# The low part of a weight piece on GpSimd: four instructions of a quarter of the columns in place of one

## The chip, the cores and the metric

The kernel runs on one core of one Trainium2 chip. The metric is the device time of one execution in microseconds (us), as the median of several runs. Engine names follow the profile: PE is TensorE's matmul, PEld its weight load, DVE is VectorE, ACT is ScalarE, POOL is GpSimd, SP is SyncE.

## The reference

256 tokens of width 1024 pass through one hybrid block (gated linear attention beside sliding-window attention, then a SwiGLU layer) and two more layers (latent attention beside an HGRN2 scan, then a dense SwiGLU in the first and a top-2-of-8 mixture of experts in the second). Cut to what matters here, the work is a chain of products with large weights, all in float32:

```
proj = h @ w_in[l]                      # 1024 x 6688, later 1024 x 2752 in each of two layers
y    = o_gla @ w_o_gla, o_swa @ w_o_swa, merged @ w_out
x    = x + (silu(h2 @ w_gate) * (h2 @ w_up)) @ w_down
...
f = lb + (1.0 - lb) * jax.nn.sigmoid(z)
log_f = jnp.log(jnp.maximum(f, F_FLOOR))
```

## The kernel before, in words

**Three passes for a float32 product.** A weight w is split into a high part, w rounded to the fp32r type, and a low part, w minus the high part. The left side is split in the same way, and PE adds up three products (L726 high by high, L727 high by low weight, L728 low by high weight). One *piece* is 128 partitions by 1024 words, as a rule two blocks of 512 columns; PE multiplies it in 12 matmuls.

**Who does what for a piece.** SP loads a weight block of 2048 words into one of four slots of the tile `arena`. ACT copies a piece to `w_hi_sb` (function `split_to`, L1519), after PE has counted up `w_used` for the piece four places before, since `w_hi_sb` and `w_lo_sb` have four buffers. Then the low part is made: on DVE for the first pieces and for nearly all of the two SwiGLU stages (L1983) and the experts (L1971), and on POOL (L655) for the 134 pieces of the mixers and of the joins between stages. PE waits for the counter of the piece (`lo_count`) before its first matmul. So a piece of the mixers goes SP, ACT, POOL, PE, and POOL may be at most three pieces ahead of the one that PE works on.

**What else the engines do there.** DVE and ACT run the elementwise work of the mixers in an order written out by hand. ACT's copies stand in that order too: behind an activation that waits for DVE, the next piece's high part waits as well. The steps which the prediction names are, in the first block, L2050 and L2069 to L2072 (rotation and norms of the attention's heads; ACT's L1573 waits for L2050), and in the two later layers the forget gate: L1938, L2356 and L2357 in the first of them, L1938, L2361, L1926, L2364, L2365, L2366, L2368 and L2370 in the second. There PE's L1137 (the running sum of the log gates) waits for L2368, PE's L860 (the turned keys) for L2370, and ACT's L1714 for L2365, with four copies of weight pieces behind it.

**The loop on POOL.** After its small loads POOL goes through the pieces with one wait and one instruction each:

```
w = raw(j)
k, n = w.shape[1:]
pool.wait_ge(sem("w_hi_ready"), hi_count[j])
pool.tensor_tensor(buffer(w_lo_sb, j, k, n), w, buffer(w_hi_sb, j, k, n).bitcast(F32),
                   ALU.subtract).then_inc(sem("w_lo_by_gpsimd"), 1)
```

Of the kernel before, what the change touches and what calls it, by code (L numbers as in the profile page):

```python
# [28 lines left out]
ALU = mybir.AluOpType  # L29
ACT = mybir.ActivationFunctionType  # L30
F32 = mybir.dt.float32
# [36 lines left out]
MOE_SUBS = 2 * MOE_LOADS  # L68
FF_UNIT = 256
FFN_UNITS = D_FF // FF_UNIT  # L70
SCRATCH = 4 * SLOT
WORK = 13952

# [113 lines left out]
def build(nc, A, out):  # L187
    gemm_at, jobs = {}, 0
    for name, _, _, width, _ in gemm_plan():
        if name in ("FFN", "lr"):  # L190
            continue
        halves = [name.replace("wo", f"wo{i}") for i in range(2)] if width == D else [name]
        for part in halves:
            gemm_at[part], jobs = jobs, jobs + T
    pair_at, pair_end, n = {}, {}, 0
# [16 lines left out]
    for name, weight, start, width, k in gemm_plan():  # L212
        if name != "FFN":
# [15 lines left out]
            else:  # L229
                n = KD if KD * width <= SUB else KD // 2  # L230
# [3 lines left out]
        down = A[f"{weight}_down"].rearrange("(k p) n -> p k n", p=P)  # L234
        for u in range(FFN_UNITS + 1):
            if u < FFN_UNITS:
                for kind in ("gate", "up"):
# [16 lines left out]
    for j, (_, _, piece) in enumerate(subs):  # L254
        by_vector = j < FIRST_SUBS or any(lo + BUFFERS <= j < hi + AFTER_FFN for lo, hi in ffn_range.values())
        maker = "w_lo_by_vector" if by_vector else "w_lo_by_gpsimd"
        if piece is not None:
            made["w_hi_ready"] += 1
            made[maker] += 1
        hi_count.append(made["w_hi_ready"])  # L260
        lo_count.append((maker, made[maker]))
# [3 lines left out]
    for j, (i, _, piece) in enumerate(subs):  # L265
        load_freed[i] = lo_count[j] if piece is not None else ("w_used", j + 1)

    with ExitStack() as ctx:
        sems = {}

        def sem(name):
            if name not in sems:
                sems[name] = ctx.enter_context(nc.semaphore(name))
            return sems[name]

        def sb(name, words, dtype=F32):
            return ctx.enter_context(nc.sbuf_tensor(name, [P, words], dtype))


        arena = sb("arena", DENSE_SLOTS * SLOT + SCRATCH + WORK)  # L280
        x_sb = sb("x_sb", T * D)
        h_sb = sb("h_sb", T * D)
        left_sb = sb("left_sb", 2 * KD * TOKENS, F32R)
        w_hi_sb, w_lo_sb = (sb(f"w_{n}_sb", BUFFERS * SUB, F32R) for n in ("hi", "lo"))
# [8 lines left out]
        def room(at, words):  # L293
            assert at + words <= SCRATCH + WORK
            at += DENSE_SLOTS * SLOT
            return arena[:, at:at + words]

        def work(at, words):
            assert at + words <= WORK
            at += DENSE_SLOTS * SLOT + SCRATCH  # L300
            return arena[:, at:at + words]

        def scratch(at, words):
            assert at + words <= SCRATCH
            return arena[:, DENSE_SLOTS * SLOT + at:DENSE_SLOTS * SLOT + at + words]
# [13 lines left out]
        def raw(j):  # L319

            i, _, piece = subs[j]
            return piece_of(slot(slot_of[i], *loads[i][1:]), piece)

        def buffer(store, j, k, n):

            at = (j % BUFFERS) * SUB
            return store[:, at:at + k * n].rearrange("p (k n) -> p k n", k=k)
# [120 lines left out]
        def wide(u):  # L448
            return 2 <= u < FFN_UNITS - 1

        def added_ahead(tag):
            return (FFN_UNITS - 3) * (tag == "f2")

# [166 lines left out]
        def _(pool):  # L620
# [29 lines left out]
            for j, (_, _, piece) in enumerate(subs):  # L650
                if piece is not None and lo_count[j][0] == "w_lo_by_gpsimd":
                    w = raw(j)
                    k, n = w.shape[1:]
                    pool.wait_ge(sem("w_hi_ready"), hi_count[j])
                    pool.tensor_tensor(buffer(w_lo_sb, j, k, n), w, buffer(w_hi_sb, j, k, n).bitcast(F32),  # L655
                                       ALU.subtract).then_inc(sem("w_lo_by_gpsimd"), 1)

            pool.wait_ge(sem("expert_gain_landed"), 16)
            for half in range(2):
# [63 lines left out]
        def _(pe):  # L723
# [308 lines left out]
            def ffn(tag, norm, turn_next):  # L1032
# [54 lines left out]
                def banks_free(u, kind):  # L1087
# [3 lines left out]
                    elif wide(u):  # L1091
                        pe.wait_ge(sem(("gate_added", "up_added")[kind]), added_ahead(tag) + u - 2)
                    elif u == FFN_UNITS - 1 and kind == 0:
                        pe.wait_ge(sem("gate_added"), added_ahead(tag) + u - 2)

                for u in range(FFN_UNITS):
                    if u == 0:
# [1619 lines left out]
```

## Time and profile before

| | |
|---|---|
| median of 3 runs | 1897.99 us (1897.94 to 1900.1) |
| the profiled execution's own time | 1899.83 us |
| span of its instructions | 1897.9 us |
| PE busy | 1875.3 us (99%) |
| DVE busy | 1523.3 us (80%) |
| ACT busy | 1240.1 us (65%) |
| POOL busy | 403.3 us (21%) |
| mean granted TensorE clock | 0.999 |

The span is from the first to the last instruction of the profiled execution. An engine's busy time counts an instruction from its start to its end, and what it spends waiting for access to memory inside the instruction counts as busy. Matmul ends are modelled, so that PE's small gaps tell more than its share. POOL works on weight pieces from 28.7 us to 278 us, from 460 to 606 us and from 787 to 922 us; in between and after that DVE makes the low parts.

### The profile page before, as it was taken

What the parts mean: (1) busy time and instruction counts of PE and PEld (TensorE: products, weight loads), DVE (VectorE), ACT (ScalarE), POOL (GpSimd) and SP (SyncE); (2) the same over time, 40 slices, a digit from 0 to 9 for tenths busy, and PEclk for the clock granted to TensorE, in tenths of its full rate; (3) what the DMA queues carried; (4) which work ended last, traced back from release to release, by engine and by line L of the source; (5) the groups of instructions that cost most, each with busy time, mean ns of one, the idle gap of its engine ahead of it and who ended that gap; (6) DMA issues with size and microseconds to landing.
All of it is one profiled execution on the core that took longest, in us unless ns stands there. A gap on an engine that the chain in (4) does not pass through costs nothing.

```text
span 1897.9 us, 26327 instructions
## 1 busy us (share of the span) xinstructions
PE 1875.3 (99%) x9450; PEld 1578.4 (83%) x9450; DVE 1523.3 (80%) x1649; ACT 1240.1 (65%) x1484; POOL 403.3 (21%) x206
## 2 busy tenths in 40 slices
PE   9999999999999999999999999999999999999997
PEld 6888888888898888878888888888888888888886
DVE  6745367777576887697699999999999999999997
ACT  6654444444644444464488888888888888888876
POOL 6856870001824000282450000000000000000000
PEclk9999999999999999999999999999999999999999
DMA  9534556665434676534599999999999999999994
GB/s 284 170 119 134 178 186 218 224 221 172 142 122 133 206 242 221 163 120 134 176 383 395 391 380 376 386 397 368 389 365 388 396 365 388 366 387 396 370 395 188
DMA packets 251397, 523.68 MB, mean 276 GB/s; under 512 B 9944, under 2 KB 58720, under 8 KB 251184
## 3 DMA queue, kind: packets, MB, share of 16 engines
q1 hardware_dynamic: 243408, 504.00, 74.2%
q10 hardware_dynamic: 5680, 11.61, 1.7%
q0 software_dynamic: 2224, 6.95, 1.1%
q8 instruction: 52, 0.85, 0.2%
q14 instruction: 33, 0.27, 0.0%
HBM read 507.19 MB, written 15.34 MB: 275 GB/s over the span
## 4 chain that ended last, share of the span: by engine, by line
PE 93%; DVE 3%; POOL 1%; ACT 1%; issue 1%; DMA 0%; SPq 0%; DVEq 0%; ACTq 0%
PE bank L726 25%; PE bank L728 24%; PE bank L727 24%; PE bank L1081 6%; PE bank L1084 3%; PE bank L1160 2%; POOL w_lo_sb L655 1%; PE bank L849 1%; PE bank L1345 1%; PE bank L822 1%; PE bank L828 1%; DMA arena<-in_w_in 0%; PE bank L990 0%; PE bank L967 0%; DVE arena L2050 0%
## 5 line engine op out<-in xcount | busy, mean ns | idle before, releaser
L1971 DVE TENSOR_TENSOR w_lo_sb<-arena,w_hi_sb 128x1024 fp32r<-128x1024 f32 x672 | 807.8, 1223 | 73.8 <-ACT w_hi_sb L1499 43.6
L1499 ACT ACTIVATE w_hi_sb<-arena 128x1024 fp32r<-128x1024 f32 x672 | 711.2, 1062 | 168.7 <-PE bank L728 168.0
L726 PE MATMUL bank<-w_hi_sb,left_sb 128*128 128x512 f32 (+1 forms) x1400 | 553.4, 395 | 2.8 <-POOL w_lo_sb L655 2.8
L728 PE MATMUL bank<-w_hi_sb,left_sb 128*128 128x512 f32 (+1 forms) x1400 | 542.3, 387 | 0.0
L727 PE MATMUL bank<-w_lo_sb,left_sb 128*128 128x512 f32 (+1 forms) x1400 | 541.5, 387 | 0.0
L1519 ACT ACTIVATE w_hi_sb<-arena 128x1024 fp32r<-128x1024 f32 (+1 forms) x269 | 278.2, 1052 | 299.8 <-PE bank L728 220.8
L655 POOL TENSOR_TENSOR w_lo_sb<-arena,w_hi_sb 128x1024 fp32r<-128x1024 f32 (+1 forms) x134 | 341.6, 2569 | 552.0 <-ACT w_hi_sb L1519 551.2
L726 PEld LDWEIGHTS bank<-w_hi_sb,left_sb 128*128 128x128 f32 x1400 | 263.1, 188 | 61.1 <-POOL w_lo_sb L655 7.6
L728 PEld LDWEIGHTS bank<-w_hi_sb,left_sb 128*128 128x128 f32 x1400 | 262.9, 188 | 54.9
L727 PEld LDWEIGHTS bank<-w_lo_sb,left_sb 128*128 128x128 f32 x1400 | 263.4, 188 | 50.9 <-issue 0.7
L726 PE MATMUL bank<-w_hi_sb,hid_hi_sb 128*128 128x512 f32 x656 | 257.3, 392 | 0.1
L727 PE MATMUL bank<-w_lo_sb,hid_hi_sb 128*128 128x512 f32 x656 | 255.6, 390 | 0.0
L728 PE MATMUL bank<-w_hi_sb,hid_lo_sb 128*128 128x512 f32 x656 | 255.5, 389 | 0.0
L1983 DVE TENSOR_TENSOR w_lo_sb<-arena,w_hi_sb 128x1024 fp32r<-128x1024 f32 x135 | 160.4, 1217 | 77.8 <-ACT w_hi_sb L1519 76.7
L710 POOL DMA_INDIRECT h_sb<-returned,arena x2 | 2.7, 1356 | 819.7 <-DMA returned<-arena 819.4
L728 PEld LDWEIGHTS bank<-w_hi_sb,hid_lo_sb 128*128 128x128 f32 x656 | 123.1, 188 | 25.9
L726 PEld LDWEIGHTS bank<-w_hi_sb,hid_hi_sb 128*128 128x128 f32 x656 | 123.3, 188 | 24.9 <-DVE w_lo_sb L1971 0.5
L727 PEld LDWEIGHTS bank<-w_lo_sb,hid_hi_sb 128*128 128x128 f32 x656 | 123.3, 188 | 24.2
L1081 PE MATMUL bank<-left_sb,w_hi_sb 128*128 128x512 f32 x512 | 127.8, 391 | 0.0
L1081 PEld LDWEIGHTS bank<-left_sb,w_hi_sb 128*128 128x128 f32 x512 | 93.1, 189 | 17.3
L1926 DVE TENSOR_TENSOR arena<-arena 128x512 f32<-128x512 f32 (+3 forms) x85 | 80.6, 948 | 27.0 <-ACT arena L1530 20.9
L1084 PEld LDWEIGHTS bank<-left_sb,w_lo_sb 128*128 128x128 f32 x512 | 69.8, 190 | 6.4 <-DVE w_lo_sb L1983 1.4
(356 smaller groups left out, 1687.5 us busy)
## 6 DMA issues: line engine op xcount, KB each, us to landing
arena<-in_moe_w_gate SPq DMA_DIRECT2D x112, 1024.0 KB, 7.9
arena<-in_moe_w_up SPq DMA_DIRECT2D x112, 1024.0 KB, 8.0
arena<-in_moe_w_down SPq DMA_DIRECT2D x112, 1024.0 KB, 7.7
arena<-in_w_in SPq DMA_DIRECT2D x45, 1024.0 KB, 5.1
arena<-in_w_ffn_in SPq DMA_DIRECT2D x22, 1024.0 KB, 5.1
arena<-in_w_out SPq DMA_DIRECT2D x12, 1024.0 KB, 5.1
arena<-in_w_ffn_out SPq DMA_DIRECT2D x11, 1024.0 KB, 4.8
arena<-in_dense_w_gate SPq DMA_DIRECT2D x11, 1024.0 KB, 5.4
```

The source lines that it names most:

```text
L655: pool.tensor_tensor(buffer(w_lo_sb, j, k, n), w, buffer(w_hi_sb, j, k, n).bitcast(F32), ALU.subtract).then_inc(sem("w_lo_by_gpsimd"), 1)
L726: pe.matmul(out, still[0], moving[0], start=start, stop=False)
L727: pe.matmul(out, still[0], moving[1], start=False, stop=False)
L728: return pe.matmul(out, still[1], moving[0], start=False, stop=stop)
L1081: pe.matmul(sums, w_hi[:, k, :], left_both[:, :, k, :], start=(k == 0), stop=False)
L1084: mm = pe.matmul(sums[:, 0, :], w_lo[:, k, :], left_hi[:, k, :], start=False, stop=(k == KD - 1))
L1160: mm = pe.matmul(b[:, i * P:(i + 1) * P], key[:, at:at + P], query[:, at:at + P], start=True, stop=True)
L1499: act.activation(expert_buffer(w_hi_sb, j), expert_piece(j % MOE_SUBS), ACT.Copy) \
L1519: act.activation(buffer(w_hi_sb, j, *w.shape[1:]), w, ACT.Copy).then_inc(sem("w_hi_ready"), 1)
L1926: dve.tensor_tensor(dst, one, two, ALU.mult).then_inc(sem(name), 1)
L1971: dve.tensor_tensor(expert_buffer(w_lo_sb, j), expert_piece(j % MOE_SUBS), expert_buffer(w_hi_sb, j).bitcast(F32), ALU.subtract) \
L1983: dve.tensor_tensor(buffer(w_lo_sb, j, *w.shape[1:]), w, buffer(w_hi_sb, j, *w.shape[1:]).bitcast(F32), ALU.subtract) \
```

## The change

`LO_CUTS = 4` is new. In POOL's loop the last dimension of a piece, n, is cut into four steps, and each step gets a subtraction of its own on the same slices of `w_lo_sb`, `arena` and `w_hi_sb`. The wait stands before the first of the four, and the counter `w_lo_by_gpsimd` goes up with the last. Nothing else changes.

```
+LO_CUTS = 4
...
                     pool.wait_ge(sem("w_hi_ready"), hi_count[j])
-                    pool.tensor_tensor(buffer(w_lo_sb, j, k, n), w, buffer(w_hi_sb, j, k, n).bitcast(F32),
-                                       ALU.subtract).then_inc(sem("w_lo_by_gpsimd"), 1)
+                    step = n // LO_CUTS
+                    for at in range(0, n, step):
+                        lo, whole, hi = (a[:, :, at:at + step] for a in (buffer(w_lo_sb, j, k, n), w, buffer(w_hi_sb, j, k, n)))
+                        ins = pool.tensor_tensor(lo, whole, hi.bitcast(F32), ALU.subtract)
+                    ins.then_inc(sem("w_lo_by_gpsimd"), 1)
```

POOL's program before, where its loads end and the pieces begin (a row is a line of the kernel, an operation, out<-in, the shape, and how many follow each other):

```order
L626 DMA level_masks<-in_level_masks 128x1024
L655 ISA
L655 TENSOR_TENSOR w_lo_sb<-arena,w_hi_sb 128x1024 x88
L655 TENSOR_TENSOR w_lo_sb<-arena,w_hi_sb 128x768 x2
L655 TENSOR_TENSOR w_lo_sb<-arena,w_hi_sb 128x1024 x30
```

The same place in the changed kernel, where the line is L659:

```order
L627 DMA level_masks<-in_level_masks 128x1024
L659 ISA
L659 TENSOR_TENSOR w_lo_sb<-arena,w_hi_sb 128x2x128 x280
L659 TENSOR_TENSOR w_lo_sb<-arena,w_hi_sb 128x8x32 x16
L659 TENSOR_TENSOR w_lo_sb<-arena,w_hi_sb 128x2x128 x56
L659 TENSOR_TENSOR w_lo_sb<-arena,w_hi_sb 128x4x48 x8
L659 TENSOR_TENSOR w_lo_sb<-arena,w_hi_sb 128x2x128 x48
```

Each piece has become four instructions, 134 pieces 536 of them, of two blocks of 128 columns as a rule; no other engine's instructions move.

## Rows read from the trace of the kernel before

**Rows 1.** The page: the span, busy times (share, count), POOL's and ACT's piece lines.

```profile
span 1897.9 us, 26327 instructions
...
PE 1875.3 (99%) x9450; PEld 1578.4 (83%) x9450; DVE 1523.3 (80%) x1649; ACT 1240.1 (65%) x1484; POOL 403.3 (21%) x206
...
L1519 ACT ACTIVATE w_hi_sb<-arena 128x1024 fp32r<-128x1024 f32 (+1 forms) x269 | 278.2, 1052 | 299.8 <-PE bank L728 220.8
L655 POOL TENSOR_TENSOR w_lo_sb<-arena,w_hi_sb 128x1024 fp32r<-128x1024 f32 (+1 forms) x134 | 341.6, 2569 | 552.0 <-ACT w_hi_sb L1519 551.2
```

**Rows 2.** Waits: who waited for whom, us in total, times, longest.

```profile
PEld bank L726 <- POOL w_lo_sb L655: 7.6, 11, 1.8
...
PE bank L726 <- POOL w_lo_sb L655: 2.8, 5, 1.4
```

**Rows 3.** Timeline of POOL (start, us, engine, line, [idle before]): long instructions, no DVE between.

```profile
28.69 9.44 POOL L655 TENSOR_TENSOR w_lo_sb<-arena,w_hi_sb 128x1024 fp32r<-128x1024 f32 x4
...
1887.14 2.52 POOL L718 TENSOR_TENSOR arena<-x_sb,arena 128x512 f32<-128x512 f32 x2 [86.67 <-DVE x_sb L2630]
```

**Rows 4.** Groups of lines: POOL's memset; timeline of POOL: an add of two columns.

```profile
L2695 POOL MEMSET const-float32-1.0<- 128x1 f32 x1 | 0.1, 98 | 0.0
...
944.02 0.20 POOL L680 TENSOR_TENSOR arena<-arena 128x2 f32<-128x2 f32 x1
```

**Rows 5.** Timeline of the second later layer's forget gate, 799 to 823 us.

```profile
799.73 14.77 POOL L655 TENSOR_TENSOR w_lo_sb<-arena,w_hi_sb 128x1024 fp32r<-128x1024 f32 x5
...
808.94 3.32 DVE L1926 TENSOR_TENSOR arena<-arena,const_sb 128x1024 f32<-128x1024 f32 x1
...
811.13 3.37 POOL L655 TENSOR_TENSOR w_lo_sb<-arena,w_hi_sb 128x1024 fp32r<-128x1024 f32 x1
...
812.30 3.29 DVE L2364 SCALAR_TENSOR_TENSOR arena<-arena,const_sb 128x1024 f32<-128x1024 f32 x1
...
814.56 0.50 PE L726 MATMUL bank<-w_hi_sb,left_sb 128*128 128x512 f32 x1 [0.32 <-POOL w_lo_sb L655]
...
818.05 1.23 DVE L2368 TENSOR_TENSOR arena<-arena 128x1024 f32<-128x1024 f32 x1
819.19 3.40 DVE L2370 TENSOR_TENSOR arena<-arena 128x1024 f32<-128x1024 f32 x1
...
819.33 2.05 PE L1137 MATMUL bank<-const_sb,arena 128*128 128x128 f32 x16 [1.73 <-DVE arena L2368]
822.64 0.33 PE L860 MATMUL bank<-const_sb,arena 128*128 128x128 f32 x1 [1.26 <-DVE arena L2370]
```

**Rows 6.** Timeline of the first later layer's forget gate, 470 to 489 us.

```profile
470.58 24.84 POOL L655 TENSOR_TENSOR w_lo_sb<-arena,w_hi_sb 128x1024 fp32r<-128x1024 f32 x9 [6.04 <-ACT w_hi_sb L1519]
...
473.70 0.50 PE L726 MATMUL bank<-w_hi_sb,left_sb 128*128 128x512 f32 x1 [0.39 <-POOL w_lo_sb L655]
...
485.03 3.37 POOL L655 TENSOR_TENSOR w_lo_sb<-arena,w_hi_sb 128x1024 fp32r<-128x1024 f32 x1
...
488.46 0.50 PE L726 MATMUL bank<-w_hi_sb,left_sb 128*128 128x512 f32 x1 [0.32 <-POOL w_lo_sb L655]
```

**Rows 7.** Timeline of the first block's start, 32 to 53 us.

```profile
32.18 6.51 DVE L2050 TENSOR_SCALAR arena<-arena 128x1024 f32<-128x1024 f32 x1
...
43.33 20.00 POOL L655 TENSOR_TENSOR w_lo_sb<-arena,w_hi_sb 128x1024 fp32r<-128x1024 f32 x7 [5.20 <-ACT w_hi_sb L1519]
...
45.95 0.50 PE L726 MATMUL bank<-w_hi_sb,left_sb 128*128 128x512 f32 x1 [1.42 <-POOL w_lo_sb L655]
...
52.10 0.50 PE L726 MATMUL bank<-w_hi_sb,left_sb 128*128 128x512 f32 x1 [0.31 <-POOL w_lo_sb L655]
```

**Rows 8.** Busy times in a stretch: us, PE, PEld, DVE, ACT, POOL (count), clock, DMA.

```profile
206.00:278.00 72.00, 72.00 (x355) 60.33 (x353) 33.69 (x33) 33.59 (x43) 63.20 (x25) 1.00 0.53 179
```

**Rows 9.** Chain of waits: one matmul of a piece, when nothing holds PE up.

```profile
580.14 0.23 PE bank L728
```

**Rows 10.** Timeline: a tiny POOL instruction beside low parts on DVE.

```profile
956.81 5.06 POOL L680 TENSOR_TENSOR arena<-arena 128x2 f32<-128x2 f32 x1
...
957.19 4.62 DVE L1971 TENSOR_TENSOR w_lo_sb<-arena,w_hi_sb 128x1024 fp32r<-128x1024 f32 x4
```

## The prediction, before the changed kernel had run

> **What bounds the kernel now.** I read the page first [rows 1]: PE is busy for 1875.3 of 1897.9 us, POOL for only 21%. So the time is PE's own work plus its gaps, and the change, which touches POOL alone, counts only where it opens or closes a gap in PE. The list of waits comes next [rows 2]: PE and its weight loads wait for POOL's low part L655 for 2.8 and 7.6 us, at some ten places, so POOL is late now and then. The mean of L655 is 2569 ns [rows 1], but a piece with no DVE work beside it takes less: four in a row take 9.44 us, 2.36 each [rows 3]. What lies between is the thing to see, and the timeline shows it. In the forget gate of the last layer a POOL piece takes 3.37 us and DVE's 1024-column instructions with two operands in SBUF take 3.29 to 3.40 us, where the same kind (L2368), met when POOL is idle, takes 1.23 [rows 5]. The sums fit taking turns: 3.29 is 1.2 of its own and 2.1 of waiting for the end of POOL's instruction; 3.37 is 2.36 and 1.0 of waiting for DVE's. So such instructions of DVE and POOL's shut each other out, whole instruction by whole instruction. The last thing to see is where PE starts a piece the moment POOL ends it: at 45.95 and 52.10 us [rows 7], at 473.70 and 488.46 us, where the piece that began at 485.03 with 3.37 us ends at 488.40 [rows 6], and at 814.56 us, where the row 799.73 + 14.77 ends at 814.50 [rows 5]. There anything added to POOL is added to PE.
>
> **Price of the four instructions.** Two L718 of 512 columns take 2.52 us, 1.26 each, against 2.36 for 1024 [rows 3]: 1.10 us for 512 columns is 2.15 ns a column, which leaves 0.16 us for the instruction itself. A quarter then takes 256 x 2.15 ns + 0.16 = 0.71 us, and a piece 2.84: **0.48 us more**. The bounds: from the memset of one column, 0.10 us, three more give +0.30; from the add of two columns, 0.20 us, +0.60 [rows 4]. Below that lies nothing added, if quarters without a wait between them run into each other; no row excludes it. I take 0.48, since L718 is the nearest in kind and size. As for the page: the Trainium skill (GPSIMD Engine Reference, Elementwise — side-by-side cycle accounting) gives 4497 ns for 2048 columns. With the 2.36 us of this trace that would be 2.09 ns a column and an estimated 0.22 us an instruction, so +0.67 us a piece and an estimated 3.4 us more over the 18 or so late pieces below than by my price.
>
> **Where it is hidden.** 134 pieces x 0.48 = 64 us more of POOL, nearly all beside other work. PE needs 12 x 0.23 = 2.7 us a piece [rows 9]. POOL may be three pieces ahead: after PE frees a buffer, ACT takes 1.05 us [rows 1] and POOL 2.4, and PE gets there three pieces later, 8.2 us, so the lead is 4.7 us. The tightest long stretch is 206 to 278 us with POOL busy for 63.2 of 72 us in 25 pieces [rows 8]. 25 x 0.48 = 12 makes that 75.2, 3.2 us too many, inside the lead: nothing. At +0.60 it is 78.2, and 1.5 us would show. If that cover is gone, every further 0.1 us per piece costs 2.5 us here.
>
> **Place A, first block.** POOL's four first pieces end at 38.13 (28.69 + 9.44), and DVE's L2050, which wanted in at 32.18, ends at 38.69 [rows 3, 7]; ACT behind it and then the piece that POOL begins at 43.33 wait on that. If L2050 stays out until POOL is through again, all of this comes 4 x 0.48 = 1.9 us later, and the three pieces until PE's start at 52.10 add 1.4: +3.3. If it gets in between quarters, POOL is no longer idle from 38 to 43 us, but has seven pieces in a row, 7 x 2.84 = 19.9 from 28.69, and the turns of L2050, L2069 to L2072 of both halves inside them (1.0 each for 1024 columns, about 0.5 for 512 and for L2050, some 6.5 in all by then): 55.1 instead of 52.05, +3.0. Both come to about **+3**.
>
> **Place B, first later layer.** Six pieces between POOL's start at 470.58 and 488.41, each of them awaited by PE or nearly so [rows 6]. DVE's turns there stay the same in number, so 6 x 0.48 = **+2.9**.
>
> **Place C, second later layer.** Six pieces end at 814.50, the five of the row and one directly before it, with three turns of DVE in them [rows 5]. Now L2364 and what is behind it (L2365, L2366, L2368, L2370) wait 0.7 us at most each instead of 2.1, so DVE runs its chain some 3 us sooner. But POOL then still has its pieces to do and gives a turn of 1.0 us to each: five turns that used to fall into POOL's pause fall into its work. The last of the six pieces ends 6 x 0.48 + 5 x 0.98 = 7.8 us later, at 822.3. PE takes 2.7 us for it and starts L1137 at 825.1 instead of 819.33; its own wait of 1.73 us for L2368 is gone, and so is that of 1.26 for L2370 before L860, which starts at about 827.0 instead of 822.64: **+4.4**. What is late next here is POOL, no longer DVE. ACT's copies behind L1714 come sooner, but POOL has no time for them.
>
> **Sum.** 3.0 + 2.9 + 4.4 = +10.3 us, after 922 us nothing. On the profiled execution's own 1899.83 that is 1910.1; that execution lies 1.8 above the median of the runs, so on the median's 1897.99 it is **1908.3 us**. With +0.30 a piece the same working gives 2.1 + 1.8 + 3.3 = 7.2, with +0.60 it gives 4.2 + 3.6 + 5.1 + 1.5 = 14.4.
>
> **Rival 1: POOL does not let DVE in between quarters** that follow each other without a wait. For it: DVE does just this to POOL when its instructions overlap; an add of two columns stood for 5.06 us beside four of DVE's [rows 10]. Against it: POOL's pieces of before follow each other without a pause too, and DVE gets in between them [rows 5]. Then A costs 3.3 and B 2.9. At C four instructions of DVE on the chain wait 0.48 longer, and L860 comes 2.4 us later: +8.6, 1906.6 us.
>
> **Rival 2: the extra price is near nothing and only the turns move.** Then A and B cost under 1, and C 5 x 0.98 less the 3.0 us that PE stood for DVE: +1.9. In all about +2.5, 1900.5 us, no change that can be told. Against it stands L718.
>
> **Rival 3: faster, because DVE is freed.** The waits of 2.1 us in DVE's chain at C shrink to 0.7 and the one of 5.9 in L2050 at A goes. If POOL kept its pace, PE would lose its gaps of 1.73 and 1.26 at C and 1.42 and 0.31 at A: -4.7, 1893.3 us. It decides at C: the sixth piece must be done 2.7 us before 819.33, by 816.6, which leaves 2.1 us for six times the extra price and five turns. It speaks for it that ACT's copies wait on this chain too; against it that turns alone take 4.9. The Trainium skill has a rule for this (SBUF — State Buffer, Who interferes with whom): a DVE instruction with two SBUF inputs contends with a reading GpSimd instruction, and who holds the pair has it for its whole instruction. By that rule shorter instructions free DVE sooner, as here; the trace agrees on the whole instruction (3.29 us beside POOL, 1.23 without it).
>
> **Rival 4: a quarter costs more than 0.85 us**, so that a piece takes 3.4 and POOL cannot keep up from 206 to 278 us: A 6, B 6, C 8 and 25 x 1.0 + 63.2 - 72 - 4.7 = 12 there: +32 or less. Only strided quarters could do that; no row shows it.
>
> **Chances.** My sum, +5 to +15: 0.66. Rival 1: 0.12. Rival 2: 0.12. Rival 3: 0.06. Rival 4: 0.04. A measurement of this kernel can tell about 0.2%, 3.8 us, from no change. Slower by more than that: 0.66 + 0.12 + 0.03 of rival 4, less a little for a sum at its lower bound, 0.79. Within it: rival 2 and the rest, 0.15. Faster: 0.06. The range that holds it 8 times in 10 goes from rival 2's 1900.0 to 1915.0, a little above the upper bound of the price.
>
> **What would show it.** Right: 536 instructions of L659 with 0.7 us each where DVE is idle, start to start, 2.8 us a piece; waits of PE for POOL up from 10 to some 20 us; L2364 and L2370 at 1.3 to 1.9 us in place of 3.3; the waits of L1137 and L860 for DVE gone; PE's start after the sixth piece at C about 14 us behind its old place when A and B are counted (3 + 2.9 + 7.8). Wrong: PE waiting for POOL no longer than before, quarters start to start at 0.6 us, or DVE's instructions still at 3.3 us, which would be rival 1.

## The result, and the profile after

The changed kernel takes **1930.7 us**, the median of four runs (1927.1 to 1940.9), against 1898.0 for the kernel before (1897.9 to 1900.1): the ratio is 1.0177, with a 95% interval from 1.0162 to 1.0192. That is 32.7 us slower, where 10.3 were predicted; the time lies outside the range. The profiled execution is the fastest of the four, 1927.1 us. In what follows, line numbers from 655 on stand 4 higher in the changed kernel than in the kernel before (L655 is L659, L1926 is L1930), and 3 to 9 higher in the kernels of the experiments (L1926 is L1929 to L1935 there).

The page first, the lines that answer to [rows 1]:

```profile
span 1925.1 us, 26729 instructions
...
PE 1882.7 (98%) x9450; PEld 1582.9 (82%) x9450; DVE 1510.7 (78%) x1649; ACT 1241.0 (64%) x1484; POOL 467.6 (24%) x608
...
L730 PE MATMUL bank<-w_hi_sb,left_sb 128*128 128x512 f32 (+1 forms) x1400 | 555.4, 397 | 12.8 <-POOL w_lo_sb L659 12.7
...
L659 POOL TENSOR_TENSOR w_lo_sb<-arena,w_hi_sb 128x256 fp32r<-128x256 f32 (+1 forms) x536 | 406.0, 799 | 515.1 <-ACT w_hi_sb L1523 515.0
```

POOL's low parts grew from 341.6 to 406.0 us, by 64.4, where 64 was predicted. That the two agree so closely is partly luck: the price measured below, 0.42 us a piece, gives 56 for 134 pieces, and the other 8 were not traced. The span grew by 27.2, though, and PE is busy for 7.4 us longer with the same 9450 matmuls. The waits (who, for whom, us in total, times, longest) show a line that has no counterpart in [rows 2]:

```profile
PEld bank L730 <- POOL w_lo_sb L659: 20.6, 18, 3.1
...
PE bank L730 <- POOL w_lo_sb L659: 13.7, 12, 2.7
...
PE bank L730 <- DVE hid_lo_sb L1960: 7.7, 1, 7.7
```

The waits for POOL went from 10.4 to 34.3 us and not to 20, and there is one wait of 7.7 us for **DVE**, on which nothing in the prediction rests. Where it comes from is seen in the timelines of POOL and of DVE around it (start, us, engine, line, [idle before]):

```profile
209.77 31.25 POOL L659 TENSOR_TENSOR w_lo_sb<-arena,w_hi_sb 128x256 fp32r<-128x256 f32 x45
...
220.94 21.16 DVE L1930 TENSOR_TENSOR arena<-arena 128x1024 f32<-128x1024 f32 x1 [5.06 <-ACT arena L1534]
242.14 0.69 DVE L1959 CAST hid_hi_sb<-bank 128x512 fp32r<-128x512 f32 x1
242.86 0.69 DVE L1960 TENSOR_TENSOR hid_lo_sb<-bank,hid_hi_sb 128x512 fp32r<-128x512 f32 x1
...
245.04 1.22 DVE L1930 TENSOR_TENSOR arena<-arena 128x1024 f32<-128x1024 f32 x1
```

One DVE instruction that takes 1.22 us by itself stands for 21.16 us. The quarters of POOL follow each other without a pause, the 45 shown and 27 before them, until 241.02, and the instruction ends 1.1 us after that: it was passed over at 29 ends of a quarter, one after the other, and let in after the row's last. The same happened at 512 us to two instructions of L2399 (9.49 us instead of 1.29), and there PE waited for the DVE copy behind them:

```profile
512.15 9.49 DVE L2399 TENSOR_TENSOR arena<-arena 128x512 f32<-128x512 f32 x2
521.56 1.40 DVE L1926 COPY arena<-bank 128x512 f32<-128x512 f32 x2
523.00 1.29 DVE L2399 TENSOR_TENSOR arena<-arena 128x512 f32<-128x512 f32 x2
...
523.02 3.22 PE L1164 MATMUL bank<-arena 128*128 128x128 f32 x14 [3.48 <-DVE arena L1926]
```

The last piece is the clock. In the kernel before it is at 1.00 until 1890 us. In the changed kernel it is not (us, busy times of PE, PEld, DVE, ACT and POOL with counts; then the granted clock of TensorE, the DMA share, GB/s):

```profile
230.00:235.00 5.00, 5.00 (x24) 4.14 (x23) 5.00 (x1) 3.10 (x4) 5.00 (x8) 1.00 0.56 210
235.00:240.00 5.00, 1.02 (x5) 0.52 (x3) 5.00 (x1) 1.06 (x1) 5.00 (x8) 0.99 0.65 209
240.00:245.00 5.00, 1.30 (x3) 1.14 (x4) 4.86 (x5) 0.00 (x0) 1.02 (x2) 0.50 0.55 176
245.00:250.00 5.00, 5.00 (x20) 3.98 (x20) 1.23 (x2) 1.06 (x1) 0.67 (x1) 0.83 0.09 34
250.00:255.00 5.00, 5.00 (x24) 4.14 (x23) 1.96 (x2) 3.10 (x4) 5.00 (x7) 1.00 0.00 0
...
520.00:530.00 10.00, 6.98 (x32) 6.38 (x33) 8.04 (x11) 5.03 (x8) 3.23 (x5) 0.83 0.19 60
...
830.00:840.00 10.00, 5.23 (x15) 3.50 (x13) 9.27 (x6) 4.62 (x6) 10.00 (x7) 0.83 0.33 105
840.00:850.00 10.00, 10.00 (x49) 8.60 (x50) 1.38 (x2) 3.68 (x4) 10.00 (x15) 0.83 0.34 88
```

While PE stands still for 7.7 us, the granted clock falls to 0.50, the lower of its two levels (1.2 GHz). It is there by 240 us and stays until 3 us after PE's start at 243.70, and in these 3 us a matmul takes 0.43 us in the chain of waits instead of the 0.23 of [rows 9]:

```profile
245.32 0.43 PE bank L730
...
247.18 0.23 PE bank L732
```

Setting each matmul's start beside the same one's before gives the account of the 27.1 us by which PE ends later (rounded): place A 2.9; the stretch from 206 to 300 us 10.0 (a gap of 7.8, 1.5 of half clock, and 0.7 at its end); place B 2.6; L2399 and the half clock behind it 5.4; place C 5.5; after it 0.8. The three places of the prediction sum to 11.0.

Place C, to be set beside [rows 5]:

```profile
829.37 1.65 DVE L1930 TENSOR_TENSOR arena<-arena,const_sb 128x1024 f32<-128x1024 f32 x1
831.05 1.63 DVE L2368 SCALAR_TENSOR_TENSOR arena<-arena,const_sb 128x1024 f32<-128x1024 f32 x1
...
837.62 1.75 DVE L2374 TENSOR_TENSOR arena<-arena 128x1024 f32<-128x1024 f32 x1
...
833.32 0.50 PE L730 MATMUL bank<-w_hi_sb,left_sb 128*128 128x512 f32 x1 [2.69 <-POOL w_lo_sb L659]
840.00 0.50 PE L730 MATMUL bank<-w_hi_sb,left_sb 128*128 128x512 f32 x1 [2.08 <-POOL w_lo_sb L659]
847.16 1.95 PE L1141 MATMUL bank<-const_sb,arena 128*128 128x128 f32 x16
848.94 1.04 PE L864 MATMUL bank<-const_sb,arena 128*128 128x128 f32 x8
```

Here DVE does what was predicted (3.3 us shrank to 1.6 to 1.75), L1141 and L864 no longer wait for it, and PE waits for POOL instead.

### The profile page after: what moved, and what is told of

It reads as the page before. It is cut to its first block, busy times and chain, and to the rows that moved or that the text cites. A ratio compares the mean times of both kernels' runs of the same rounds, so it can differ in the third digit from the quotient of the medians.

```text
span 1925.1 us, 26729 instructions
## 1 busy us (share of the span) xinstructions
PE 1882.7 (98%) x9450; PEld 1582.9 (82%) x9450; DVE 1510.7 (78%) x1649; ACT 1241.0 (64%) x1484; POOL 467.6 (24%) x608
## 4 chain that ended last, share of the span: by engine, by line
PE 87%; POOL 6%; DVE 4%; ACT 1%; issue 1%; DMA 0%; SPq 0%; DVEq 0%; ACTq 0%; POOLq 0%
PE bank L730 23%; PE bank L732 23%; PE bank L731 23%; PE bank L1085 6%; POOL w_lo_sb L659 5%; PE bank L1088 3%; PE bank L1164 1%; DVE arena L1930 1%; PE bank L1349 1%; PE bank L826 1%; PE bank L853 1%; PE bank L832 1%; DMA arena<-in_w_in 0%; ACT w_hi_sb L1523 0%; POOL small_sb L624 0%
## 5 line engine op out<-in xcount | busy, mean ns | idle before, releaser
L659 POOL TENSOR_TENSOR w_lo_sb<-arena,w_hi_sb 128x256 fp32r<-128x256 f32 (+1 forms) x536 | 406.0, 799 | 515.1 <-ACT w_hi_sb L1523 515.0
L1930 DVE TENSOR_TENSOR arena<-arena 128x512 f32<-128x512 f32 (+3 forms) x85 | 90.2, 1061 | 20.3 <-ACT arena L1534 14.1
```

What stands on the lines that cost most here:

```text
L659: ins = pool.tensor_tensor(lo, whole, hi.bitcast(F32), ALU.subtract)
L1930: dve.tensor_tensor(dst, one, two, ALU.mult).then_inc(sem(name), 1)
```

## The experiments

The theory at first: the price and the three places are right, and what comes on top is DVE, shut out by a row of POOL instructions without a pause, plus the clock that falls behind PE's gaps. The first rival: quarters that are all alike keep DVE out, by their rhythm; the second: the stretch from 206 to 278 us is simply too full for POOL.

**The changed kernel again**, unchanged.

> The changed kernel once more, to see its spread. Theory S (DVE is shut out by an unbroken row of quarters until POOL runs dry, and whether it happens is decided anew in each execution): the single times spread over 5 us or more, where the kernel before spreads over 2, and this profile has its DVE instructions of over 5 us at other lines than 2091, 1930 and 2399, or of other length. Rival P (the added price per piece and the turns make all of it, and DVE's long instruction is a fixed consequence of that): the same instructions stand as long as in the first profile, and the times agree within 0.3%. Both: ratio 1.012 to 1.022.

Measured: 1938.0 us (1930.4 to 1939.2), ratio 1.0189 (1.0171 to 1.0207). Its profiled execution (span 1937.0) has a second long row in DVE's timeline:

```profile
220.27 21.16 DVE L1930 TENSOR_TENSOR arena<-arena 128x1024 f32<-128x1024 f32 x1 [5.06 <-ACT arena L1534]
244.36 1.22 DVE L1930 TENSOR_TENSOR arena<-arena 128x1024 f32<-128x1024 f32 x1
252.48 1.63 DVE L1930 TENSOR_TENSOR arena<-arena 128x1024 f32<-128x1024 f32 x1 [6.90 <-ACT arena L1534]
264.26 12.63 DVE L1930 TENSOR_TENSOR arena<-arena 128x1024 f32<-128x1024 f32 x1 [2.34 <-ACT arena L1534]
```

The first is the same to 0.01 us. The one at 264.26 is not in the first execution, and costs PE another gap of 8 us with half clock behind it. So an instruction may get in (252.48) or not (264.26), and that differs between executions: it accounts for most of the 12 us between the two profiled ones (PE loses 20.2 us here between 206 and 300 us, 10.0 in the first). Place A cost 2.1 us here. The runs of this kernel spread over 14 us, those of the kernel before over 3.

**A chain of quarters**: POOL waits after each of a piece's first three quarters for that quarter's own completion.

```diff
+                        if at + step < n:
+                            parts[0] += 1
+                            ins.then_inc(sem("w_lo_part"), 1)
+                            pool.wait_ge(sem("w_lo_part"), parts[0])
```

> Each of the first three quarters of a piece counts up a semaphore and POOL waits for it before the next, so that POOL lets go between quarters. It costs more per quarter: about 0.1 us, 3.1 to 3.3 us a piece. Theory S: no DVE instruction of before 960 us stands longer than 2.5 us more than alone, TensorE's clock stays at 1.0 in all stretches, and what is lost is price and turns: with +0.85 a piece some 6 + 5 + 7 us at the three places and 8 us from 206 to 278 us, 1924 us. Rival P: the same, and in addition at least as many long stops of DVE as in the changed kernel, over 1935 us.

Measured: 1932.7 us, ratio 1.0175 (1.0161 to 1.0189). No DVE instruction beside POOL takes more than 2.7 us, so with these waits there are no long holds. But a piece now takes 3.15 us, and PE lost some 14.5 us in the stretch that has the 206 to 278 us of before in it. The only engine that PE waited for there is POOL; in the whole kernel its two lists of waits for POOL name 38.9 and 24.4 us. The time is 9 us over what was expected, and speaks for the second rival. The granted clock fell as well, to 0.83 in several windows of 10 us, without one long gap.

**Halves instead of quarters** (LO_CUTS = 2).

> Two halves in place of four quarters. Measured in the changed kernel: 2.77 us a piece against 2.36, 0.14 for each further instruction, so 2.50 here. POOL has 63.2 + 25 x 0.14 = 66.7 us of work in the 72 from 206 to 278 us and pauses in between. Theory S: with pauses DVE is not shut out for long, and the loss is 1 + 1 at the first two places and 3 at the third: 1903 us. Rival P: linear in the number of instructions, a third of the changed kernel's 33 us: 1909 us.

Measured: 1901.8 us, ratio 1.0014 (1.0005 to 1.0023), 2.9 us over the kernel before on the same chip. A piece takes 2.50 us where DVE is idle. With 2.35 for one instruction and 2.78 for four, an instruction more costs 0.14 to 0.15 us.

**Uneven cuts**: three slivers (2 of the columns in each of the views, 4 elements a partition) and the rest.

```diff
-                    for at in range(0, n, step):
+                    for at, to in ((0, 2), (2, 4), (4, 6), (6, n)):
```

> Four instructions a piece again, but cut at columns 2, 4 and 6 of each block: three tiny ones and one with nearly all the columns. The price per piece stays (2.7 to 2.9 us), and the piece is given to DVE in steps of about 2.3 us as before. Theory S: POOL is as full as with quarters, so DVE can be shut out here too, about as often: 1915 to 1930 us. If instead the short even quarters are what shuts DVE out, no DVE instruction stands over 5 us, and the time is the price alone at the three places, 1906 to 1910 us. Rival P: as the changed kernel without its further turns, 1920 us or more with no DVE instruction over 5 us.

Measured: 1926.8 us, ratio 1.0146 (1.0130 to 1.0161). DVE's timeline:

```profile
233.43 2.19 DVE L1929 TENSOR_TENSOR arena<-arena 128x1024 f32<-128x1024 f32 x1 [5.09 <-ACT arena L1533]
244.31 14.46 DVE L1929 TENSOR_TENSOR arena<-arena 128x1024 f32<-128x1024 f32 x1 [8.70 <-ACT arena L1533]
```

So the shutting out doesn't come of quarters that are alike; the first rival falls. A piece takes 2.79 us here, and up to this hold PE had lost nothing in the stretch.

**A pause ahead of each piece**: POOL waits for its own completion of the piece before.

```diff
+                    if lo_count[j][1] > 1:
+                        pool.wait_ge(sem("w_lo_by_gpsimd"), lo_count[j][1] - 1)
```

> Quarters as in the changed kernel, but before each piece POOL waits for the end of its own last quarter: one small pause a piece (about 0.13 us, 2.9 us a piece) in place of none. Theory S (an unbroken row of POOL instructions shuts a DVE instruction out until POOL runs dry; a pause lets it in): no DVE instruction is held for more than about 3 us, the 14 us that the changed kernel's first profile lost behind L1930 and L2399 are gone although each piece costs more, and the sum of price and turns is 3.5 + 3.5 + 6 us: 1911 us, from 1908 to 1916. Rival P (what was lost is POOL's time, so more per piece costs more): as long as the changed kernel or longer, over 1930 us.

Measured: 1919.8 us, ratio 1.0110 (1.0094 to 1.0125). No DVE instruction beside POOL takes more than 2.7 us, and DVE's L1932 (L1930 above) takes 1.55 to 1.73 us all four times in the stretch. That is 11 us better than the change. Yet it missed what was expected of it, 1908 to 1916 us: PE still loses 7.5 us from 206 us to the end of the stretch (7.1 if counted to 300 us). So with one pause a piece no long hold is left in this trace, and something else remains. The pause is not where DVE gets in, though: three of these four L1932 were let in at the end of a quarter behind which POOL does not wait.

**Quarters only for pieces 40 to 73** (the middle stretch), and **quarters for all but these**.

```diff
+                    step = n // (LO_CUTS if 40 <= number[0] < 74 else 1)
+                    number[0] += 1
```

> Quarters only for POOL's pieces 40 to 73, those of about 178 to 278 us; all others are whole. Theory S: DVE's L1930 is shut out there as in the changed kernel (21 us, in some executions a second time for 12), and this stretch alone makes 10 to 20 us of the loss: 1908 to 1919 us. Theory of my prediction (this stretch is covered by POOL's lead): 1899 us.

> The complement: whole pieces 40 to 73, all others in quarters. Theory S with my three terms: what the changed kernel's first profile lost outside of that stretch, 2.9 + 2.6 + 5.1 (L2399 shut out after the second place) + 5.7 + about 1: 1915 us. Rival P, by the share of the pieces (100 of 134 of the changed kernel's 33 to 39 us): 1923 us or more.

Measured: 1910.5 us, ratio 1.0060 (1.0044 to 1.0075), and 1918.4 us, ratio 1.0110 (1.0094 to 1.0126). Over the kernel before that is 11.6 and 19.5 us, together 31.1 of the change's 33 to 39. The second is 3 us over what was expected, and one of its four runs took 1924.6; in its profiled execution place A cost 4.2 us, since L2050 (L2056 there) stood for 7.54 us. In the first L1932 stands for 21.15 us again, and the waits of its stretch from 205 to 312 us name DVE for nearly all that PE lost:

```profile
PE bank L732 <- DVE hid_lo_sb L1962: 7.7, 1, 7.7
...
PE bank L732 <- POOL w_lo_sb L661: 0.8, 1, 0.8
```

**Halves for the first eight pieces only.**

> Two halves for POOL's first eight pieces, all others whole. In the kernel with two halves everywhere PE stood 1.3 us ahead of its old place at 58 us, since DVE's rotation is let in sooner, and lost that later. If the two parts are independent, the gain stays: 1896.5 to 1897.5 us, 1.3 us under the kernel before. If not, or if the gain hangs on later pieces, 1898 to 1899 us.

Measured: 1899.5 us, ratio 1.0004 (0.9995 to 1.0013). L2050 of the first block (L2056 here), which stood for 6.51 us [rows 7], took 0.93; L2069 (L2075 here), shortly behind it, took 5.90 instead. PE was 1.9 us ahead at the seventh piece and kept 1.0 of it in the profiled execution; no difference can be timed, and the 1896.5 to 1897.5 us that a kept gain would have given did not come.

Then three kernels for the question that the pause left open: what costs PE 7.5 us in the middle when DVE gets in?

**Quarters and pauses for pieces 40 to 73 only**, and **for pieces 50 to 73 only**.

> Quarters only for pieces 40 to 73, and ahead of each of these pieces POOL waits for its own completion of the piece before; every other piece is one instruction, with no such wait. Theory (the lost lead: POOL is nearly level with PE at pieces 42 and 43 and a piece of 2.90 us can't win the lead back): no DVE instruction is held for more than 3 us, and PE still loses 6 to 8 us in the stretch, as in the kernel with quarters and pauses everywhere: 1904 to 1907 us. Rival (what quarters cost in this stretch is only DVE shut out by a row of quarters without a pause, 11.9 us before, and the clock that falls after it): then next to nothing is lost once DVE gets in, 1898 to 1900 us.

> The same with quarters and pauses only for pieces 50 to 73. POOL's lead over PE in the kernel before is 5.3 us at piece 50, against 1.1 at piece 43. Theory (the lead decides): a lead of 4 to 5 us takes up most of 24 pieces at 0.55 us more than before; PE loses 0 to 3 us, 1898 to 1901 us, less than half of the kernel with pieces 40 to 73. Rival (each piece of 2.90 us costs PE its share, whatever the lead): 24/34 of what the kernel with pieces 40 to 73 loses, some 5 us, 1903 us.

Measured: 1907.1 us, ratio 1.0042 (1.0025 to 1.0059), and 1903.8 us, ratio 1.0025 (1.0016 to 1.0035): 8.1 and 4.8 us over the kernel before. In the kernel from piece 40 on the clock is 0.998, it is at its full level in every window of 10 us between 20 and 1000 us, and no DVE instruction of the stretch is held. What holds PE is POOL alone, here in the waits from 205 to 312 us and in the shares of the chain from 225 to 250 us:

```profile
PEld bank L734 <- POOL w_lo_sb L663: 8.5, 9, 2.1
PE bank L734 <- POOL w_lo_sb L663: 5.6, 6, 1.7
...
by line: POOL w_lo_sb L663 98.7%; issue 1.7%; POOLq L658 0.5%
```

The chain runs over POOL, so the lead that the prediction counted on is used up here. The trace of the kernel before shows why. POOL's pieces 42 and 43, its line first, fall beside two 2048-column instructions of DVE, and PE's start on piece 43 follows 1.1 us after POOL has done it:

```profile
184.53 8.35 POOL L655 TENSOR_TENSOR w_lo_sb<-arena,w_hi_sb 128x1024 fp32r<-128x1024 f32 x2 [4.01 <-ACT w_hi_sb L1519]
...
183.91 2.29 DVE L1926 TENSOR_TENSOR arena<-arena,small_sb 128x2048 f32<-128x2048 f32 x1
186.24 4.38 DVE L1926 TENSOR_TENSOR arena<-arena,h_sb 128x2048 f32<-128x2048 f32 x1
...
194.01 0.39 PE L726 MATMUL bank<-w_hi_sb,left_sb 128*128 128x512 f32 x1
```

From there a POOL that takes 2.35 us a piece against PE's 2.72 wins the lead back: 2.3, 3.6, 4.0, 4.4 and 5.6 us at pieces 44 to 48. From piece 49 to piece 71 it is 3.8 to 5.4 us. With quarters and pauses (2.90) it is 0.2 at piece 43, gets no further than 1.8, and is gone at piece 56; from there PE waits.

The kernel that starts at piece 50 has 4.8 us of lead there. Its PE loses nothing until 245 us, when that is used up, and then 5.1 us by the end of the stretch. So the lead does hide what it is worth, and decides where the loss begins; but the expected 0 to 3 us was too low, and the rival's 5 is the number that came out. The reason is at the other end: PE takes the last pieces of the stretch in 1.4, 2.2 and 1.5 us each instead of 2.7, and so the lead is down to 1.4 us at piece 73 in the kernel before already.

**The kernel before with a pause ahead of each piece**, its low parts uncut.

> The kernel before, each low part one instruction, but ahead of each piece POOL waits for its own completion of the piece before. What the pause costs alone: 0.12 us a piece as measured between the kernels with quarters. Theory: L2050 at the first block gets in at the first boundary instead of after three; three late places of 4 to 6 pieces cost 0.5 to 0.7 us each: 1899 to 1901 us, no difference that can be told. Rival (the freed DVE is worth more at the first block than the pauses cost): 1895 to 1898 us.

Measured: 1899.7 us, ratio 1.0004 (0.9995 to 1.0014): no difference that can be told. In the first block DVE gets in at the first end of a piece (L2056 is L2050 of [rows 7]):

```profile
28.95 4.93 POOL L661 TENSOR_TENSOR w_lo_sb<-arena,w_hi_sb 128x1024 fp32r<-128x1024 f32 x2
34.40 5.71 POOL L661 TENSOR_TENSOR w_lo_sb<-arena,w_hi_sb 128x1024 fp32r<-128x1024 f32 x2 [0.53 <-ACT w_hi_sb L1525]
...
32.41 2.01 DVE L2056 TENSOR_SCALAR arena<-arena 128x1024 f32<-128x1024 f32 x1
```

That wins 2.3 us there, and the pauses cost 1.4 later; what would be left can't be timed. No version that was run beats the kernel before.

## Why the prediction was wrong

- **Price of the four instructions: right.** Predicted 2.84 us a piece; measured 2.78 (45 quarters in 31.25 us, 0.69 each). The price of an instruction more is 0.14 to 0.15 us, near the 0.16 from L718 and not the 0.22 estimated from the Trainium skill (GPSIMD Engine Reference, Elementwise — side-by-side cycle accounting).
- **Place A: right.** +3 predicted, +2.9 measured, and of the two ways the second: L2054 took 1.38 us, and POOL had no pause any more. How that either/or falls was not known ahead, and it is not worth the same either way: in two other executions with quarters there, place A cost 2.1 and 4.2 us.
- **Place B: right.** +2.9 predicted, 2.6 measured.
- **Place C: right in mechanism, a little low.** +4.4 predicted, 5.5 measured. The turns fell as said, POOL took DVE's place as the last one awaited, and PE's start after the sixth piece came 9.0 us later within this place instead of 7.8; half clock between 833 and 844 us adds to it.
- **"Where it is hidden": the step that failed.** It put all of the stretch from 206 to 278 us at nothing because POOL would be 3.2 us too long in it and 4.7 us ahead. Three things are wrong in that. First, DVE was shut out by the row that POOL's work had become, and PE waited 7.7 us for it. Second, the half clock after it, 1.5 us. These two make nearly all of the 10.0 us that the changed kernel loses here; only 0.7 at the end of the stretch is waiting for POOL. The other profiled execution pays for a second gap of 8 us. Third, the cover itself: 4.7 us is near what POOL has in the middle of the stretch (3.8 to 5.4 us at pieces 49 to 71), but it is 1.1 at piece 43, just ahead of the stretch, and 1.4 at piece 73, its end, and a row of work can be late only by what is left at its end. By the prediction's own numbers, 3.2 less 1.4, an estimated 1.8 us should have shown. With pauses, and DVE never held, the stretch costs 7.5 us (pieces 40 to 73). That sum has the pauses' own 0.12 us a piece in it: what the lead alone would cost at 2.78 us a piece, no kernel shows, and the changed one had lost nothing in the stretch before DVE was shut out. A POOL that can't keep up and a DVE that is shut out don't add up: while DVE is held, it takes no turns from POOL, which gets ahead.
- **A term that was missing**: L2399 at 512 us, 5.4 us, the same shutting out. The prediction had no term between B and C.
- **Rival 1** had the mechanism, that POOL doesn't let DVE in between its quarters, but priced it as one piece of waiting (0.48 us more) where it can be the whole rest of the row: up to 21.16 us. The evidence was there. L2050's 6.51 us [rows 7] runs over three ends of whole pieces, until POOL's row is through, and I took it as a case by itself. The evidence against it, that DVE gets in between pieces at place C [rows 5], is true too, and still is with quarters; both happen. The rule of the Trainium skill (SBUF — State Buffer, Who interferes with whom), that the holder has the pair for its whole instruction, fits the turns of 1.6 us; being passed over at 29 ends of instructions is more than it states.
- **Rivals 2 and 3** fell by the price. **Rival 4** named the right stretch and a POOL that can't keep up, but asked for 0.85 us a quarter. With the pauses, at 2.90 us a piece (0.72 a quarter), POOL could not keep up; for 0.69 no run shows it.

What stays open: which end of an instruction DVE wins. Most instructions get in at the first. Most of those that didn't stayed out until POOL's row ended, but not all: in three executions L2399 was let in at the fifth end, with eight more quarters of the row to come (the row is POOL's, 864.67 to 882.66 us; the first of the two L2399 takes 3.69 us of the 4.83):

```profile
864.67 17.99 POOL L659 TENSOR_TENSOR w_lo_sb<-arena,w_hi_sb 128x192 fp32r<-128x192 f32 x24 [3.34 <-ACT w_hi_sb L1523]
...
872.62 4.83 DVE L2399 TENSOR_TENSOR arena<-arena 128x512 f32<-128x512 f32 x2
```

Neither the evenness of the quarters nor cutting as such decides it (L2050 is held with uncut pieces). In the traces of the three kernels where POOL waits for its own completion throughout, no DVE instruction was held in this way, so the pauses remove the long holds. How they do it is not shown, since in the kernel with quarters and one pause a piece DVE gets in mostly at ends without one, and neither is why an attempt is lost.

## What to carry to other kernels

A lead must be read where it is used: how long after the producer's end the consumer starts, piece by piece, at the start, the tightest point and the end of the stretch: work that gets longer all through a stretch is late by what its end leaves, whatever the lead in the middle. A slower producer also loses the rate at which it would win a lead back. When GpSimd's work is cut into smaller instructions, every pause that it has lost counts, for a DVE instruction that meets a row without one may stand until the row ends. Look for a single DVE instruction in the trace of the kernel before that took several times its own length, and take the rest of the row as the upper bound of its price.

## What the runs showed of the hardware

- A DVE instruction with 1024 columns stood for 21.16 us (1.22 alone) beside GpSimd instructions of 0.69 us without a pause, passed over at 29 ends of them, and for the same 21.16 and 21.15 us in two other executions. It ended 1.1 us after the row. One with 512 columns was let in at the fifth end, before the row was through, in three executions.
- A semaphore wait of GpSimd on its own last instruction costs about 0.12 us (2.78 to 2.90 us a piece; 3.15 with three of them), and in the three kernels that had it throughout no long hold was seen: DVE was let in at the first end of a GpSimd instruction, also where no wait stood behind it.
- TensorE's granted clock fell to its lower level in a gap of 7.7 us and behind one of 3.5 us, and also where PE stood for 2 to 3 us several times close together (0.83 in the 10 us from 830). In the stretch of the kernel with pauses for pieces 40 to 73, whose longest wait for POOL is 2.1 us, it stayed up. At the lower level a matmul of 0.23 us took 0.43.
